# Gate weights and residual rows loaded before the scatter's wait, split before the last silu, and two token tiles transposed from finished rows

## The chip, the cores and the metric

The kernel runs on one core of a Trainium2 chip. The metric is the device time of one execution in microseconds (us). One core has TensorE (PE), VectorE (DVE), ScalarE (ACT), GpSimd (POOL) and SyncE (SP), which here only issues DMA transfers; 16 DMA engines move the data.

## The reference

One hybrid decoder layer on 512 tokens of width 1024, in float32:

```python
h = rms_norm(x, g_mix[i]); proj = h @ w_in[i]
# conv branch and block-sparse attention, normalised, concatenated, projected
x = x + mixed @ w_out[i]                                   # x1
x = x + hier_moe(rms_norm(x, g_ffn[i]), ...)               # x2; top-2 of 8 experts in the top-1 of 4 groups
gate = jax.nn.sigmoid(rms_norm(x, g_ple[i]) @ w_ple_gate[i] + b_ple_gate[i])
x = x + (p[i] @ w_ple_proj[i]) * gate                      # x3
return rms_norm(x, g_final)
# each expert: silu(h @ w_gate[e]) * (h @ w_up[e]) @ w_down[e], with F = 256
```

The change lies where the experts end and the gate product (x2 @ w_ple_gate, 1024 by 1024) begins.

## The kernel before

Every engine has its own program, written out by hand, and semaphores join them; the order of the instructions on an engine is the order in the source.

*Experts.* A tile is 128 rows of gathered tokens, 96 of one expert (a = 0) and 32 of another (a = 1). For tile n TensorE multiplies by the gate and up weights (L1987), ScalarE takes the silu (L1023), VectorE multiplies by the up half (L1567), TensorE turns the result (L2008), ScalarE copies it out (L1028), TensorE multiplies by the down weights (L2017), and ScalarE (L1031) and VectorE (L1573) copy the two halves of the result into yb. GpSimd scatters yb to y_d in memory (L818), by token and by which of its two experts it was. Weights stream into two slots of wring; SP reloads a slot's up weights (L607) when its up product is done, and the down weights (L635) when its down product is done. `before` is the index of the last pair of tiles, so that tile 2 * before + 1 is the last.

*What follows them.* x2 = x1 + gw0 * y0 + gw1 * y1 for four token tiles t. For t = 0 and 1 (BY_PASS) the part of the last expert tile doesn't go through memory: SP loads what y_d holds once the scatter of tile 2 * before is done (`early`, L738), VectorE adds it to x1 to give xp (add_early, L1554), and TensorE adds the last tile's share straight from yb, with a matrix share_of[t] that picks and weighs its rows. turn_and_add gives x2 of such a tile transposed, as 8 pairs of a matmul with the identity (L2077) and one with share_of (L2078); add_in_rows gives the share in rows (L2087), and VectorE adds xp (rows_out, L1604) to give x2 in rows in xs. For t = 2 and 3 (LATE) the last scatter must be done; its issue on POOL waits for the early loads to have landed, since these read what it overwrites. SP then loads yg (L751), VectorE adds twice (add_last, L1554), and TensorE transposes xs (turn_x2, L2064).

*The gate product.* product(q, lo, hi) does passes lo to hi of quantity q (q = half * 4 + t): wpg_hi times x2_hi, wpg_hi times x2_lo, wpg_lo times x2_hi, eight matmuls each (L2052). ScalarE makes wpg_hi (split_gate, L1014) and x2_hi (high_out, L1050), VectorE wpg_lo (L1590) and x2_lo (low_out, L1611). The gate weights of half 0 are loaded in two halves of 1 MB over the up weights of slot 0 (L740), x1 comes back from memory as two pairs of token tiles (L729 and L741), and half 1 of the gate weights follows (L743). Behind the last expert tile 36 turns of the identity keep TensorE occupied (L2090). Behind the product come, for each q, the sigmoid, the multiply with the p projection, the add to xs, and for the later half the final norm and the store.

Of the kernel before, what the change touches and what calls it, by code (L numbers as in the profile page):

```python
# [28 lines left out]
F32 = mybir.dt.float32  # L29
# [7 lines left out]
P = 128  # L37
# [23 lines left out]
BY_PASS = (0, 1)  # L61
LATE = (2, 3)
# [161 lines left out]
def build(nc, x, w_in, w_out, w_r, w_gate, w_up, w_down, w_pg, w_pp, pT, b_pg, g_final, prm, cst, out):  # L224
    ctx = ExitStack()
    with ctx:
# [323 lines left out]
        def _(sp):  # L550
# [179 lines left out]
            sp.wait_ge(down_done, 2 * last_pair + 1)  # L730
            sp.sem_inc(sp_go, 1)
            sp.wait_ge(y_stored[0], 16 * half)
# [6 lines left out]
            for kh, loaded in enumerate((pg_half, pg_loaded[0])):  # L739
                sp.dma_start(wpg[0][:, 4 * kh:4 * kh + 4], pg[:, 4 * kh:4 * kh + 4, 0:512]).then_inc(loaded, 16)  # L740
            sp.dma_start(xs[:, 2:4], x1_rows[:, 2:4]).then_inc(x1_loaded[1], 16)  # L741
# [102 lines left out]
        def _(act):  # L844
# [172 lines left out]
            def one(n, s, h, made, prior=None):  # L1017
                prior = n - 1 if prior is None else prior
                for q in made[:1]:
                    ple_out(q)  # L1020
                act.wait_ge(up_done, n + 1)
# [22 lines left out]
            one(2 * before + 1, 1, before, MADE_LAST[1], 2 * before)  # L1044
# [17 lines left out]
            split_gate(0, 0, 4)  # L1062
            high_out(0)
            split_gate(0, 4, DK)
# [51 lines left out]
        def _(dve):  # L1116
# [440 lines left out]
            def add_early(t):  # L1557

                if t == 0:
                    dve.wait_ge(x1_loaded[0], 16)  # L1560
                for k in range(2):
                    add_rows(xp[:, t, :], xs[:, t, :], early[:, 2 * t + k, :], early_loaded[t], t, k, xp_ready, 2 * t + k)

            def one(n_, s, h, last, prior):
                dve.wait_ge(sil_ready, n_ + 1)
# [3 lines left out]
                if not last:  # L1569
                    x_out(n_ + 1, 1 - s, n_)  # L1570
# [14 lines left out]

            def split_gate(h):

                for k in range(DK):
                    dve.wait_ge(whi_ready, h * DK + k + 1)
                    dve.scalar_tensor_tensor(out=wpg_lo[h][:, k, :], in0=wpg[h][:, k, :], scalar=pr[:, Q_PLE + k:Q_PLE + k + 1],  # L1590
                                             in1=wpg_hi[h][:, k, :].bitcast(F32), op0=ALU.mult,
                                             op1=ALU.subtract).then_inc(wlo_ready, 1)
# [22 lines left out]
            add_early(0)  # L1615
            add_early(1)
            low_out(0)
            rows_out(0)
            split_gate(0)
            low_out(1)  # L1620
            rows_out(1)
# [5 lines left out]
            split_gate(1)  # L1627
# [65 lines left out]
        def _(pe):  # L1693
# [363 lines left out]
            def turn_x2(t):  # L2057
                pe.wait_ge(x2_ready, 2 * LATE.index(t) + 2)
                for kh in range(2):
                    name = ("x2", t, kh)  # L2060
# [6 lines left out]
            def turn_and_add(t):  # L2067

                pe.wait_ge(xp_ready, 2 * t + 2)
                for kh in range(2):  # L2070
                    name = ("x2", t, kh)
                    banks.wait_free(pe, name)
                    if t == 0:
                        pe.wait_ge((ya_ready, yd_ready)[kh], 2 * before + 2)
                    for k in range(4):
                        cols = slice((4 * kh + k) * P, (4 * kh + k + 1) * P)
                        pe.matmul(bk(name)[:, k * P:(k + 1) * P], xp[:, t, cols], ident, start=True, stop=False)  # L2077
                        ins = pe.matmul(bk(name)[:, k * P:(k + 1) * P], yb[:, 1, cols], share_of[t], start=False, stop=True)  # L2078
                    filled(ins, name)

            pe.wait_ge(xgT_ready, 4 * before + 4)
            def add_in_rows(t):

                for kh in range(2):
                    name = ("rows", t, kh)
                    banks.wait_free(pe, name)
                    filled(pe.matmul(bk(name)[:], share_of[t], yb[:, 1, kh * 512:(kh + 1) * 512], start=True, stop=True), name)  # L2087

            for _ in range(36):
                pe.transpose(pb[3][:, 0:P], ident, ident)  # L2090
# [42 lines left out]
```

## Time and profile before

| | us |
|---|---|
| median of 3 runs | 584.43 |
| lowest, highest | 580.81, 585.07 |
| the profiled execution | 582.8 |
| its span | 581.0 |
| TensorE busy in it | 514.4 |
| VectorE busy | 299.1 |
| ScalarE busy | 188.7 |
| DMA, 154.52 MB | mean 266 GB/s |

Times in the rows are counted from the start of the span. A row of the timeline has its start, its length, the engine, the line, the operation and, in brackets, how long the engine had stood idle and what ended that. In the answers on one line of the source the durations are in ns, min/median/max, and behind them stand the first and the last start. A landing is the time from a transfer's issue to its last part's arrival.

### The profile page before, as it was taken

The numbers are of one execution on the slowest core, as the hardware profiler recorded it, in microseconds if no ns is written. First come the engines' busy times: TensorE is split into PE (matmuls) and PEld (weight loads), VectorE is DVE, ScalarE is ACT, GpSimd is POOL, SyncE is SP. The second block draws the span as 40 slices with busy tenths as digits, with TensorE's granted clock in tenths as the row PEclk, the third lists the DMA queues.
The fourth block names the chain that finished last, engine by engine and source line by source line (L and its number), as shares of the span: only waits on it lengthen the run. The fifth ranks groups of instructions, "written<-read, shape, count | busy, mean of one in ns | idle before, by whom it ended". The sixth has DMA issues, their size and how long they took to land.

```text
span 581.0 us, 9043 instructions
## 1 busy us (share of the span) xinstructions
PE 514.4 (89%) x3313; PEld 308.3 (53%) x3313; DVE 299.1 (51%) x577; ACT 188.7 (32%) x361; POOL 78.1 (13%) x90
## 2 busy tenths in 40 slices
PE   4999999997889979988999996969989799899993
PEld 4788888774556658873333332323323223268882
DVE  4339899999996954487232111101111111059866
ACT  6821411337775352331101000101111001146675
POOL 1740000000042040010211221011110200010000
PEclk9999999999889979998999999989989989999998
DMA  9931900445506065498999999999999999596002
GB/s 316 372 130 40 394 21 16 148 158 172 213 2 272 1 260 212 151 392 302 334 395 422 417 421 417 408 386 409 414 418 397 410 397 418 213 396 253 2 36 109
DMA packets 39000, 154.52 MB, mean 266 GB/s; under 512 B 5808, under 2 KB 10416, under 8 KB 27568
## 3 DMA queue, kind: packets, MB, share of 16 engines
q1 hardware_dynamic: 33488, 143.33, 62.8%
q0 software_dynamic: 5184, 10.50, 4.9%
q8 instruction: 26, 0.43, 0.3%
q10 hardware_dynamic: 288, 0.15, 0.1%
q14 instruction: 14, 0.11, 0.1%
HBM read 142.43 MB, written 18.87 MB: 278 GB/s over the span
## 4 chain that ended last, share of the span: by engine, by line
PE 57%; DMA 21%; DVE 9%; ACT 6%; SPq 3%; issue 3%; POOL 1%; DVEq 0%; POOLq 0%; ACTq 0%
DMA wring<-w_up_in 20%; PE bank L1716 15%; PE bank L1987 13%; PE bank L2052 6%; PE bank L1818 5%; PE bank L1742 4%; PE bank L2017 3%; SPq L540 2%; SPq L607 1%; PE bank L1859 1%; PE bank L1786 1%; DVE wring L1239 1%; DVE mix L1176 1%; PE bank L1699 1%; DVE woa_lo L1226 1%
## 5 line engine op out<-in xcount | busy, mean ns | idle before, releaser
L1987 PE MATMUL bank<-wring,arena 128*32 128x512 f32 x848 | 106.7, 633 | 20.7 <-DMA wring<-w_up_in 19.5
L1176 DVE SCALAR_TENSOR_TENSOR mix<-arena,pr,mix 128x512 f32<-128x512 f32 x120 | 86.6, 792 | 0.0
L1987 PEld LDWEIGHTS bank<-wring,arena 128*32 128x32 f32 x848 | 30.9, 116 | 89.6 <-issue 78.9
L1567 DVE TENSOR_TENSOR arena<-arena,bank 128x256 f32<-128x256 f32 x16 | 6.7, 421 | 135.8 <-ACT arena L1023 135.8
L2017 PE MATMUL bank<-wring,arena 128*32 128x512 f32 x448 | 51.0, 595 | 6.8 <-ACT arena L1028 6.8
L1023 ACT ACTIVATE arena<-bank 128x256 f32<-128x256 f32 x16 | 6.1, 384 | 129.7 <-PE bank L1987 129.7
L818 POOL DMA_INDIRECT y_d<-arena,ycur x16 | 16.4, 1026 | 174.4 <-DVE arena L1573 173.4
L1573 DVE COPY arena<-bank 128x512 f32<-128x512 f32 x16 | 11.1, 692 | 54.6 <-PE bank L2017 54.6
L1716 PE MATMUL bank<-hT_hi,win_hi 128*128 128x512 f32 x128 | 33.5, 398 | 1.5 <-DVE hT_lo L1154 0.9
L2017 PEld LDWEIGHTS bank<-wring,arena 128*32 128x32 f32 x448 | 13.2, 109 | 35.2 <-issue 26.6
L1716 PE MATMUL bank<-hT_lo,win_hi 128*128 128x512 f32 x128 | 31.6, 389 | 0.0
L1716 PE MATMUL bank<-hT_hi,win_lo 128*128 128x512 f32 x128 | 31.6, 389 | 0.0
L1031 ACT ACTIVATE arena<-bank 128x512 f32<-128x512 f32 x16 | 9.6, 597 | 60.5 <-PE bank L2017 60.5
L1716 PEld LDWEIGHTS bank<-hT_hi,win_hi 128*128 128x128 f32 x128 | 23.6, 188 | 9.8 <-ACT hT_hi L872 1.9
L1716 PEld LDWEIGHTS bank<-hT_lo,win_hi 128*128 128x128 f32 x128 | 24.0, 188 | 5.0
L1716 PEld LDWEIGHTS bank<-hT_hi,win_lo 128*128 128x128 f32 x128 | 24.0, 188 | 5.0
L775 POOL TENSOR_TENSOR mixa_lo<-mix,mixa_hi 128x512 fp32r<-128x512 f32 x4 | 5.7, 1415 | 134.4 <-ACT mix L933 134.4
L1460 DVE TENSOR_TENSOR arena<-bank,pr 128x512 f32<-128x512 f32 x31 | 20.0, 687 | 5.3 <-PE bank L1950 4.9
L867 ACT ACTIVATE win_hi<-wring 128x1024 fp32r<-128x1024 f32 x20 | 20.0, 1071 | 6.5 <-DMA wring<-w_in_in 6.5
L911 ACT ACTIVATE wring<-wring,nmax 128x128 f32<-128x128 f32 (+3 forms) x32 | 17.8, 560 | 11.0 <-DVE nmax L1239 11.0
L769 POOL TENSOR_TENSOR win_lo<-wring,win_hi 128x1024 fp32r<-128x1024 f32 x8 | 18.9, 2390 | 14.7 <-ACT win_hi L867 14.7
L1950 PEld LDWEIGHTS bank<-c,arena 128*128 128x128 f32 x128 | 13.9, 140 | 12.4 <-issue 11.1
(292 smaller groups left out, 888.8 us busy)
## 6 DMA issues: line engine op xcount, KB each, us to landing
wring<-w_down_in SPq DMA_DIRECT2D x28, 1024.0 KB, 18.5
wring<-w_gate_in SPq DMA_DIRECT2D x24, 1024.0 KB, 12.7
wring<-w_up_in SPq DMA_DIRECT2D x24, 1024.0 KB, 18.3
wring<-w_in_in SPq DMA_DIRECT2D x3, 2048.0 KB, 14.4
wring<-w_in_in SPq DMA_DIRECT2D x4, 1024.0 KB, 11.6
y_d<-rt SPq DMA_DIRECT2D x1, 4096.0 KB, 18.3
wring<-w_out_in SPq DMA_DIRECT2D x2, 2048.0 KB, 9.1
wring<-y_d SPq DMA_DIRECT2D x8, 512.0 KB, 6.3
```

Source lines behind the costliest of these rows:

```text
L769: pool.tensor_tensor(win_lo[j][:, :, cols], win[j][:, :, cols], win_hi[j][:, :, cols].bitcast(F32), ALU.subtract).then_inc(win_lo_ready[j], 1)
L818: pool.indirect_dma_start(y_d, bass.IndirectOffsetOnAxis(ap=ycur[:, s:s + 1], axis=0), yb[:, s, :], None, bounds_check=2 * S - 1, oob_is_e ...
L867: act.activation(win_hi[i][:, :, cols], win[i][:, :, cols], ACT.Copy).then_inc(win_hi_ready[i], 1)
L911: act.activation(prob[:, u_ % 4, hh, 0:n], prob[:, u_ % 4, hh, 0:n], ACT.Exp, scale=-1.0, bias=nmax[:, b, hh:hh + 1], accum_out=psum_p[:, ...
L1176: ins = dve.scalar_tensor_tensor(out=mixc[:, mm, :], in0=u[:, mm, j:j + S], scalar=w, in1=mixc[:, mm, :], op0=ALU.mult, op1=ALU.add)
L1460: dve.tensor_tensor(xgT[:, s, 4 * kh:4 * kh + 4, :], pb[kh][:].rearrange("p (k n) -> p k n", k=4), pr[:, Q_FFN + 4 * kh:Q_FFN + 4 * kh + 4 ...
L1716: ins = pe.matmul(bk(name)[:], w[:, k, m * P:(m + 1) * P], h[:, k, :], start=(j == 0 and k == 0), stop=(j == 2 and k == DK - 1))
L1742: ins = pe.matmul(bk(("v", t))[:], h[:, k, t * P:(t + 1) * P], w[:, k, :], start=(j == 0 and k == 0), stop=(j == 2 and k == DK - 1))
L1818: ins = pe.matmul(bk(name)[:], src[:, m, t * P:(t + 1) * P], weight[:, m, half * 512:(half + 1) * 512], start=(j == 0), stop=(j == 3 * CM ...
L1987: ins = pe.matmul(pb[2 + s][lo:hi, :], xgT[:, s, k, lo:hi], weights[:, :, k, :], start=(k == 0), stop=(k == DK - 1))
L2017: ins = pe.matmul(pb[6 + half][lo:hi, :], hidT[:, s, k, lo:hi], dn_cols(w, a, k, half), start=(k == 0), stop=(k == FK - 1))
L2052: ins = pe.matmul(bk(name)[:], lhs, w[:, k, :], start=(j == 0 and k == 0), stop=(j == 2 and k == DK - 1))
```

## The change

SP's wait for the last but one tile becomes a wait for its up product, and behind it SP issues the two halves of the gate weights and the second pair of x1 at once, ahead of its waits for the scatters and ahead of the early y loads. ScalarE and VectorE split six of the eight slices of the first gate weights (AHEAD = 6) in the last expert tile: ScalarE in front of its wait for the up product and so in front of the silu, VectorE in front of its multiply. VectorE also does the two early adds of tile 0 between its multiply and its copy of the down result. turn_and_add and the 36 idle turns are gone; for t = 0 and 1 TensorE makes the rows first (add_in_rows), VectorE adds xp, and turn_x2 transposes the sum. TensorE's order is rows(0), turn(0), pass 1 of product 0, rows(1), passes 2 and 3, turn(1), product 1 and so on as before.

```diff
--- before.py
+++ after.py
@@ -59,6 +59,7 @@
 MADE = {8: (0,), 9: (1, 2), 10: (3,), 11: (4, 5)}
 MADE_LAST = ((6,), (7,))
 BY_PASS = (0, 1)
+AHEAD = 6
 LATE = (2, 3)
 LAST = 2 * TT - 1
 STRAIGHT = NE // 2 - 4
@@ -727,8 +728,11 @@
             last_pair = pairs_but_last(sp)
             y_rows = y_d.rearrange("(k t p) n -> p t k n", k=2, p=P)
             sp.dma_start(xs[:, 0:2], x1_rows[:, 0:2]).then_inc(x1_loaded[0], 16)
-            sp.wait_ge(down_done, 2 * last_pair + 1)
+            sp.wait_ge(up_done, 2 * last_pair + 1)
             sp.sem_inc(sp_go, 1)
+            for kh, loaded in enumerate((pg_half, pg_loaded[0])):
+                sp.dma_start(wpg[0][:, 4 * kh:4 * kh + 4], pg[:, 4 * kh:4 * kh + 4, 0:512]).then_inc(loaded, 16)
+            sp.dma_start(xs[:, 2:4], x1_rows[:, 2:4]).then_inc(x1_loaded[1], 16)
             sp.wait_ge(y_stored[0], 16 * half)
             sp.sem_inc(sp_go, 1)
             sp.wait_ge(y_stored[1], 16 * last_pair)
@@ -736,9 +740,6 @@
             for t in BY_PASS:
                 for k in range(2):
                     sp.dma_start(early[:, 2 * t + k, :], y_rows[:, t, k]).then_inc(early_loaded[t], 16)
-            for kh, loaded in enumerate((pg_half, pg_loaded[0])):
-                sp.dma_start(wpg[0][:, 4 * kh:4 * kh + 4], pg[:, 4 * kh:4 * kh + 4, 0:512]).then_inc(loaded, 16)
-            sp.dma_start(xs[:, 2:4], x1_rows[:, 2:4]).then_inc(x1_loaded[1], 16)
             banks.wait_full(sp, ("ple", 2 * TT - 1))
             sp.dma_start(wpg[1], pg[:, :, 512:D]).then_inc(pg_loaded[1], 16)
 
@@ -1014,10 +1015,13 @@
                     act.activation(wpg_hi[h][:, k, :], wpg[h][:, k, :], ACT.Copy,
                                    scale=pr[:, Q_PLE + k:Q_PLE + k + 1]).then_inc(whi_ready, 1)
 
-            def one(n, s, h, made, prior=None):
+            def one(n, s, h, made, prior=None, last=False):
                 prior = n - 1 if prior is None else prior
                 for q in made[:1]:
                     ple_out(q)
+                if last:
+                    split_gate(0, 0, 4)
+                    split_gate(0, 4, AHEAD)
                 act.wait_ge(up_done, n + 1)
                 wait(act, hid_ready, prior)
                 act.activation(sil[:, s, :], pb[2 + s][:, 0:F], ACT.Silu).then_inc(sil_ready, 1)
@@ -1041,7 +1045,7 @@
                 for s in range(2):
                     one(2 * i + s, s, i, ())
             one(2 * before, 0, before, MADE_LAST[0], 2 * number(act, halves[0:1, 2:3], PAIRS // 2 - 2, HALVES - 2) + 1)
-            one(2 * before + 1, 1, before, MADE_LAST[1], 2 * before)
+            one(2 * before + 1, 1, before, MADE_LAST[1], 2 * before, True)
 
             def high_out(t):
 
@@ -1059,9 +1063,8 @@
                     act.wait_ge(x2_ready, 2 * LATE.index(t) + 2)
                 mean_root(2, t, junk)
 
-            split_gate(0, 0, 4)
             high_out(0)
-            split_gate(0, 4, DK)
+            split_gate(0, AHEAD, DK)
             high_out(1)
             split_gate(1, 0, 4)
             for kh in range(2):
@@ -1554,19 +1557,31 @@
                 dve.scalar_tensor_tensor(out=to, in0=rows, scalar=gw[:, k, t:t + 1], in1=base if k == 0 else to,
                                          op0=ALU.mult, op1=ALU.add).then_inc(done, 1)
 
-            def add_early(t):
+            def add_early(t, ks):
 
                 if t == 0:
                     dve.wait_ge(x1_loaded[0], 16)
-                for k in range(2):
+                for k in ks:
                     add_rows(xp[:, t, :], xs[:, t, :], early[:, 2 * t + k, :], early_loaded[t], t, k, xp_ready, 2 * t + k)
 
+            def split_gate(h, lo, hi):
+
+                for k in range(lo, hi):
+                    dve.wait_ge(whi_ready, h * DK + k + 1)
+                    dve.scalar_tensor_tensor(out=wpg_lo[h][:, k, :], in0=wpg[h][:, k, :], scalar=pr[:, Q_PLE + k:Q_PLE + k + 1],
+                                             in1=wpg_hi[h][:, k, :].bitcast(F32), op0=ALU.mult,
+                                             op1=ALU.subtract).then_inc(wlo_ready, 1)
+
             def one(n_, s, h, last, prior):
+                if last:
+                    split_gate(0, 0, AHEAD)
                 dve.wait_ge(sil_ready, n_ + 1)
                 wait(dve, hidT_full, prior)
                 dve.tensor_tensor(hid[:, s], sil[:, s, :].rearrange("p (n k) -> p k n", k=FK),
                                   pb[2 + s][:, F:2 * F].rearrange("p (n k) -> p k n", k=FK), ALU.mult).then_inc(hid_ready, 1)
-                if not last:
+                if last:
+                    add_early(0, (0, 1))
+                else:
                     x_out(n_ + 1, 1 - s, n_)
                 dve.wait_ge(down_done, n_ + 1)
                 wait(dve, y_stored[s], 16 * h)
@@ -1583,14 +1598,6 @@
             one(2 * before, 0, before, False, 2 * number(dve, halves[0:1, 2:3], PAIRS // 2 - 2, HALVES - 2) + 1)
             one(2 * before + 1, 1, before, True, 2 * before)
 
-            def split_gate(h):
-
-                for k in range(DK):
-                    dve.wait_ge(whi_ready, h * DK + k + 1)
-                    dve.scalar_tensor_tensor(out=wpg_lo[h][:, k, :], in0=wpg[h][:, k, :], scalar=pr[:, Q_PLE + k:Q_PLE + k + 1],
-                                             in1=wpg_hi[h][:, k, :].bitcast(F32), op0=ALU.mult,
-                                             op1=ALU.subtract).then_inc(wlo_ready, 1)
-
             def add_last(t, k):
 
                 add_rows(xs[:, t, :], xs[:, t, :], yg[:, 2 * t + k, :], yg_loaded[t], t, k, x2_ready, 2 * LATE.index(t) + k)
@@ -1612,19 +1619,19 @@
                         x2_lo[t][:, 4 * kh:4 * kh + 4, :], bk(name)[:].rearrange("p (k n) -> p k n", k=4),
                         x2_hi[:, 4 * kh:4 * kh + 4, t * P:(t + 1) * P].bitcast(F32), ALU.subtract), name)
 
-            add_early(0)
-            add_early(1)
+            rows_out(0)
+            add_early(1, (0,))
             low_out(0)
-            rows_out(0)
-            split_gate(0)
+            add_early(1, (1,))
+            split_gate(0, AHEAD, DK)
+            rows_out(1)
             low_out(1)
-            rows_out(1)
             dve.wait_ge(x1_loaded[1], 16)
             for t in LATE:
                 for k in range(2):
                     add_last(t, k)
             low_out(2)
-            split_gate(1)
+            split_gate(1, 0, DK)
             low_out(3)
             for t in range(TT):
                 inverse(2, t)
@@ -2055,8 +2062,11 @@
                     filled(ins, name)
 
             def turn_x2(t):
-                pe.wait_ge(x2_ready, 2 * LATE.index(t) + 2)
+                if t in LATE:
+                    pe.wait_ge(x2_ready, 2 * LATE.index(t) + 2)
                 for kh in range(2):
+                    if t in BY_PASS:
+                        banks.wait_emptied(pe, ("rows", t, kh))
                     name = ("x2", t, kh)
                     banks.wait_free(pe, name)
                     for k in range(4):
@@ -2064,37 +2074,21 @@
                         ins = pe.transpose(bk(name)[:, k * P:(k + 1) * P], xs[:, t, cols], ident)
                     filled(ins, name)
 
-            def turn_and_add(t):
-
-                pe.wait_ge(xp_ready, 2 * t + 2)
+            def add_in_rows(t):
+
                 for kh in range(2):
-                    name = ("x2", t, kh)
+                    name = ("rows", t, kh)
                     banks.wait_free(pe, name)
                     if t == 0:
                         pe.wait_ge((ya_ready, yd_ready)[kh], 2 * before + 2)
-                    for k in range(4):
-                        cols = slice((4 * kh + k) * P, (4 * kh + k + 1) * P)
-                        pe.matmul(bk(name)[:, k * P:(k + 1) * P], xp[:, t, cols], ident, start=True, stop=False)
-                        ins = pe.matmul(bk(name)[:, k * P:(k + 1) * P], yb[:, 1, cols], share_of[t], start=False, stop=True)
-                    filled(ins, name)
-
-            pe.wait_ge(xgT_ready, 4 * before + 4)
-            def add_in_rows(t):
-
-                for kh in range(2):
-                    name = ("rows", t, kh)
-                    banks.wait_free(pe, name)
                     filled(pe.matmul(bk(name)[:], share_of[t], yb[:, 1, kh * 512:(kh + 1) * 512], start=True, stop=True), name)
 
-            for _ in range(36):
-                pe.transpose(pb[3][:, 0:P], ident, ident)
-            turn_and_add(0)
+            add_in_rows(0)
+            turn_x2(0)
             product(0, 0, 1)
-            add_in_rows(0)
-            product(0, 1, 2)
-            turn_and_add(1)
             add_in_rows(1)
-            product(0, 2, 3)
+            product(0, 1, 3)
+            turn_x2(1)
             for t in range(1, TT):
                 product(t, 0, 2)
                 if t < TT - 1:
```

## Rows read from the trace of the kernel before

**Rows 1.** Chain of waits from 478 us on: start, us, what.

```profile
478.72 18.64 DMA wring<-w_up_in
...
506.35 3.64 PE bank L2017 x32
509.99 4.08 PE bank L2090 x36
514.07 0.22 PE bank L2077 x2
...
521.27 1.72 PE bank L2087 x4
...
530.14 5.48 PE bank L2052 x24
535.62 0.87 PE bank L2064 x8
```

**Rows 2.** Timeline, all engines, 503 to 529 us (parts).

```profile
504.55 0.38 ACT L1023 ACTIVATE arena<-bank 128x256 f32<-128x256 f32 x1 [7.22 <-PE bank L1987]
504.96 0.42 DVE L1567 TENSOR_TENSOR arena<-arena,bank 128x256 f32<-128x256 f32 x1 [9.34 <-ACT arena L1023]
...
510.06 0.60 ACT L1031 ACTIVATE arena<-bank 128x512 f32<-128x512 f32 x1 [3.76 <-PE bank L2017]
510.06 0.69 DVE L1573 COPY arena<-bank 128x512 f32<-128x512 f32 x1 [4.67 <-PE bank L2017]
510.67 1.28 DVE L1554 SCALAR_TENSOR_TENSOR arena<-wring,gw,xs 128x1024 f32<-128x1024 f32 x1
511.50 0.49 POOL L811 COPY ycur<-tlist 128x1 int32 x1 [13.99 <-DMA wring<-y_d]
513.03 1.08 POOL L818 DMA_INDIRECT y_d<-arena,ycur  x1 [1.05 <-issue]
514.01 2.56 ACT L1014 ACTIVATE wpg_hi<-wring,pr 128x512 fp32r<-128x512 f32 x4 [3.36 <-DMA wring<-w_pg_in]
520.25 1.76 SPq L751 DMA_DIRECT2D wring<-y_d  x4
523.64 5.38 DVE L1590 SCALAR_TENSOR_TENSOR wpg_lo<-wring,pr,wpg_hi 128x512 fp32r<-128x512 f32 x8
```

**Rows 3.** Stretches: us, busy by engine, clock, DMA share, GB/s.

```profile
495.00:497.50 2.50, 1.78 (x8) 0.48 (x11) 0.62 (x1) 1.11 (x2) 0.99 (x1) 1.00 0.56 234
497.50:500.00 2.50, 2.50 (x24) 0.71 (x28) 0.00 (x0) 0.00 (x0) 0.01 (x1) 1.00 0.49 192
500.00:505.00 5.00, 4.48 (x44) 1.17 (x36) 0.04 (x1) 0.38 (x1) 0.00 (x0) 1.00 0.24 84
```

**Rows 4.** Landings: L729 (x1), L738 (early y), L740 (gate halves), a down load at 463.

```profile
L729 SPq DMA_DIRECT2D xs<-x_d x1: 388/388/388, 482.7 to 482.7; - x1
...
DMA to landing us min/median/max: 22.8/22.8/22.8
...
L738 SPq DMA_DIRECT2D wring<-y_d x4: 337/424/432, 503.8 to 505.1; - x4
...
DMA to landing us min/median/max: 3.5/4.9/6.2
...
L740 SPq DMA_DIRECT2D wring<-w_pg_in x2: 529/632/736, 505.6 to 506.4; - x2
...
DMA to landing us min/median/max: 8.4/9.5/10.5
...
wring<-w_down_in SPq DMA_DIRECT2D x1, 1024.0 KB, 23.8
```

**Rows 5.** TensorE: two up products, and the clock (0.50) in one of them.

```profile
465.34 8.77 PE L1987 MATMUL bank<-wring,arena 128*32 128x512 f32 x64 [3.92 <-DMA wring<-w_up_in]
...
481.92 7.07 PE L1987 MATMUL bank<-wring,arena 128*32 128x512 f32 x64 [0.39 <-DMA wring<-w_up_in]
...
467.00:469.00 2.00, 2.00 (x12) 0.43 (x8) 0.00 (x0) 0.00 (x0) 0.00 (x0) 0.50 0.96 397
```

More of the change, by code:

```diff
@@ L2065, in turn_x2 @@
                     filled(ins, name)
-            def turn_and_add(t):
-                pe.wait_ge(xp_ready, 2 * t + 2)
-                for kh in range(2):
-                    name = ("x2", t, kh)
-                    banks.wait_free(pe, name)
-                    if t == 0:
-                        pe.wait_ge((ya_ready, yd_ready)[kh], 2 * before + 2)
-                    for k in range(4):
-                        cols = slice((4 * kh + k) * P, (4 * kh + k + 1) * P)
-                        pe.matmul(bk(name)[:, k * P:(k + 1) * P], xp[:, t, cols], ident, start=True, stop=False)
-                        ins = pe.matmul(bk(name)[:, k * P:(k + 1) * P], yb[:, 1, cols], share_of[t], start=False, stop=True)
-                    filled(ins, name)
-            pe.wait_ge(xgT_ready, 4 * before + 4)
             def add_in_rows(t):
@@ L2086, in add_in_rows @@
                     banks.wait_free(pe, name)
+                    if t == 0:
+                        pe.wait_ge((ya_ready, yd_ready)[kh], 2 * before + 2)
                     filled(pe.matmul(bk(name)[:], share_of[t], yb[:, 1, kh * 512:(kh + 1) * 512], start=True, stop=True), name)
-            for _ in range(36):
-                pe.transpose(pb[3][:, 0:P], ident, ident)
-            turn_and_add(0)
+            add_in_rows(0)
+            turn_x2(0)
             product(0, 0, 1)
-            add_in_rows(0)
-            product(0, 1, 2)
-            turn_and_add(1)
             add_in_rows(1)
-            product(0, 2, 3)
+            product(0, 1, 3)
+            turn_x2(1)
             for t in range(1, TT):
```

## Prediction

> **What bounds the kernel now.** I read the chain of waits first, from 478 us to the end [rows 1]. Its first piece is not work of an engine but the transfer of the last expert tile's up weights, which holds everything until 497.36. Then comes the last tile on TensorE: up product, silu, product with the other half, turn, down product, ended at 509.99. From there the chain is TensorE almost without a hole: 36 idle turns (4.08 us), two tiles turned and added from xp and yb, two sets of rows, and 24 passes of the gate product. So an instruction that leaves TensorE between 510 and 572 gives its full time back, if its inputs are there; before 497 only DMA counts.
>
> Second, the timeline around the last tile [rows 2]: its silu runs on ScalarE at 504.55, the multiply on VectorE at 504.96, and neither engine has anything to do for the seven us before. That hole is where the change puts the splits. Third, the DMA share by stretches [rows 3]: full until 495, then 0.56, 0.49 and 0.24, and full again from 505. That looks like room: 2.5 x 0.44 + 2.5 x 0.51 + 5 x 0.76 = 6.2 us of all engines, or 2.5 MB at the 400 GB/s of the full stretches. Fourth, and this decides, the landings [rows 4]. The first x1 transfer (1 MB, L729) is issued at 482.7 and lands after 22.8 us, at 505.4 or 505.5 (I go on with 505.4), though the mean share has been under 0.6 for ten us. A few DMA engines are far behind the rest, and a transfer is complete only when its last part is.
>
> **The change part by part.**
>
> *Removed from TensorE.* The 36 idle turns, 4.08. turn_and_add(0) and (1): each 16 pieces of 0.22, two instructions a piece, like the first of them at 514.07 [rows 1], so 3.6 each. In their place turn_x2(0) and (1), two lots of eight transposes at 0.87 (the row at 535.62 [rows 1]), so 7.2 - 1.7 = 5.5 less. add_in_rows stays at 1.72 each.
>
> *The new head, if down ends when it does now.* Rows of yb need both copies of the down result (ScalarE to 510.66, VectorE to 510.75 [rows 2]). Then rows 1.72; VectorE adds the second half 0.69 (L1604, as the copy of the same shape at 510.06 [rows 2]); the last four transposes 0.5; ScalarE's high part 0.6; what is left of the first pass, with the splits of k 6 and 7 behind that high part (2 x 0.64), some 1.6 with the steps between. That is 5.1 plus 0.7 for the copy, 5.8 to the end of pass 1, at 515.9. Now pass 1 ends at 521.3 (the piece of rows at 521.27 starts there). Behind pass 1 there are now 23 passes x 1.82 (5.48 for three) = 41.9, rows(1) 1.72, and three turns x 0.87 = 2.6: 46.2. The last pass, ended at 571.9 in the profile, would end at 562.1: 9.8 less, before any stall. From the last pass on nothing is touched.
>
> *The moved loads.* SP now waits for the up product of the last tile but one, which ends at 488.99 [rows 5], instead of its down product, some 5.6 us on (in the last tile down ends 5.5 behind up: 509.99 against 504.5). It then issues the two 1 MB halves of the gate weights and the second x1 transfer (1 MB), all three ahead of its waits for the scatters, which end now at 503.8 [rows 4]. Behind them now stand the wait itself (nothing lost, they are issued long before), the four early y loads and the second half of the gate weights. In the queue they stand behind the x1 transfer that lands at 505.4. In the stretch after 503.8 transfers land in the order of issue: early y at 505.1 + 6.2 = 511.3, gate halves at 505.6 + 8.4 = 514.0 and 506.4 + 10.5 = 516.9 [rows 4]. The gate halves cost 2.8 each there. On the parts that are last, the same work comes behind 505.4: first half 508.2, second 511.1. Transfers do not speed up the late parts: the average share is no measure of them.
>
> By the Trainium skill (DMA: Bandwidth & Descriptors, Queues, rings and completion order) each engine consumes its own ring in order, and a DMA's count is full only when each of its engines has posted. The trace agrees: 505.4 at a share of 0.24. By that rule the sum is the one here; by the mean share alone the halves would be there by 503.5.
>
> *The splits in front of the silu.* ScalarE now waits in front of the silu for the first half (508.2; four splits, 2.56, to 510.8) and the second (511.1; two more, 1.28, to 512.4; the four at 514.01 took 2.56 [rows 2]). Queued behind them is the last silu: 512.8 instead of 504.93. VectorE's last low part (5.38 / 8 = 0.67 each, L1590 [rows 2]) ends at 513.1, its multiply at 513.55 instead of 505.38: 8.2 later. Who waits for that: TensorE's turn of hid, the down product, both copies, the scatter and all of the head. TensorE stands still for some 9 us.
>
> *The clock.* After an idle time of 3.92 us at 461.4 the granted clock fell from full (2.4 GHz) to half (1.2) at 467, and the 64 matmuls took 8.77 us instead of 7.07 [rows 5]. A 9 us hole won't cost less than that in kind; the nearest row gives 1.7. The bounds: nothing, if the fall lies wholly in the hole; 4.1, if turn (0.44) and down (3.64) all run at half. I take 1.7. By the Trainium skill (TensorE: Matmul & The Clock Gate, Why this matters for your kernels) waits on DMA between bursts lower the clock, which speaks against this change too; the row has the number.
>
> So down ends at 509.99 + 8.2 + 1.7 = 519.9, pass 1 at 525.8.
>
> *The second scatter and what hangs on it.* The early y loads (2 MB, 5.2 on the late parts) now stand behind the moved x1 transfer (2.6): 511.1 + 2.6 + 5.2 = 518.9 instead of 511.3. The last scatter waits for them (copy and issue 1.5 more [rows 2], 520.4) and for yb (520.6 and 0.9 on POOL as now): issued at 521.5. It needs 7.2 (513.03 to the y loads' issue at 520.25), so 528.7; two y loads 4.9 (median of the early ones), 533.6; VectorE's two adds 2 x 1.28, 536.2. TensorE comes to turn_x2(2) at 525.8 + 1.72 + 2 x 1.82 + 0.87 + 2 x 1.82 = 535.7. A stall of 0.5 us. VectorE's new order (rows_out(0), one add, low_out(0), the other, two splits, rows_out(1)) ends rows_out(1) near 530, before turn_x2(1) at 531.2, so it costs nothing; were it 1 us later, it would cost that. VectorE starts on the gate outputs 1.8 us nearer to the end than now, which I cost at nothing: the outputs come three passes, 5.5 us, apart [rows 1], and it has idle time between the late ones; with that cover gone it costs up to 1.8.
>
> *Sum.* 525.8 + 46.2 + 0.5 = 572.5 against 571.9: the 9.8 saved are given back as 8.2 of late splits, 1.7 of clock and 0.5 of stall, +0.6. The profiled execution has a span of 581.0 and took 582.8; the new one takes 583.4. It stood 1.6 below the median of the runs, 584.4. On that scale I predict 585.
>
> Bounds of this case: with no cost of the clock, down ends at 518.2, but the scatter is then held by the early loads, and the stall grows to 1.1: 572.0 - 0.7 = 571.3, or 583.8 on the median's scale. With 4.1: 587.4. If the late parts are 2 us less late, the whole chain is 2 us earlier: 583. So 582 to 588.
>
> **The rivals.**
>
> *A. The hole in DMA takes the loads in.* If what lags were only the x1 transfer and the moved ones ran in the free share, 2 MB would be in at 503.5, the split of k 5 done at 504.8 and the silu at most 0.4 late. Then early y lands at 511.3 as now, the scatter is done at 520.3, y at 525.2, the adds at 527.8, against TensorE at 515.9 + 0.4 + 9.9 = 526.2: a stall of 1.6. End 515.9 + 0.4 + 46.2 + 1.6 = 564.1, 7.8 less: 576.6 on the median's scale. For it: the share of 0.24. Against it: 22.8 us for x1, and 23.8 for a down load in the loop before [rows 4], which says that the lag is no single event.
>
> *B. The late parts are later still (slower).* Place: the wait for the second half, in front of the silu. If the first half, issued at 489.1, needs what that down load needed, 23.8, it lands at 512.9 and the second at 515.8, 4.7 later than in the sum. With the clock at half through all of the down product (2.4 more) the end is 0.6 + 4.7 + 2.4 = 7.7 over before: 592. It decides (over 590.3) from 5.3 us above my sum on. For it: 2 KB rows in the gate weights against 8 KB in the experts'. Against it: the same halves cost 2.8 each at 511 to 517, beside full traffic.
>
> *C. The lag is partly gone.* The halves land 3 to 5 us earlier than in my sum, and the end with them: 580 to 582, within 1% still.
>
> **How the numbers follow.** The held-back silu as summed 0.5, C 0.12, A 0.25, B 0.13. One per cent of 584.4 (about what a measurement of this kernel can tell from no change) is 5.8: faster is under 578.6, which is A, 0.25; slower is over 590.3, B, 0.13; the rest 0.62. The likeliest case gives 585; its own range is 582 to 588. To leave out no more than 2 in 10 the range reaches to A's number and to the foot of B: 577 to 591.
>
> **What would show it.** Right: a ScalarE idle time before its first split of about 10 us that ends with the gate weights' landing near 508, a second short one; the silu near 512.4; TensorE idle about 9 us before the turn of hid; a granted clock of 0.5 behind it; the span of 36 idle turns gone; turn_x2(2) waiting for less than 2 us. Wrong: the silu within 1 us of 504.6 (then A), a stall of over 3 us at turn_x2(2) (then the scatter was sized wrong), or a full clock through the down product.

## The result, and the profile after

The changed kernel takes 583.8 us in the median (582.35 to 585.93, 20 runs), the kernel before 581.5 (579.93 to 585.07, 20 runs). The ratio is 1.0035, with a 95% interval of 1.0019 to 1.0052: slower by 2.3 us between the medians and 2.0 by the ratio, a small loss that 20 runs can tell, and within 1%. The forecast was 585, range 577 to 591, and "within 1%" as the likeliest.

Chain of waits of the changed kernel from 458 us on (start, us, what):

```profile
458.87 20.38 DMA wring<-w_up_in
...
479.30 7.12 PE bank L1994 x64
...
486.50 19.17 DMA wring<-w_pg_in
...
505.69 0.73 ACT wpg_hi L1015
...
506.45 3.31 DVE wpg_lo L1571 x5
...
512.07 6.33 PE bank L2024 x32
```

Before, the chain stands on the up weights until the last tile and goes straight down the tile [rows 1]. Now it runs through the gate weights, which are no part of that tile: their transfer, ScalarE's split, VectorE's low parts, and only then the multiply and the down product.

Timeline of the changed kernel, the same stretch:

```profile
495.02 7.07 PE L1994 MATMUL bank<-wring,arena 128*32 128x512 f32 x64 [0.95 <-DMA wring<-w_up_in]
...
501.24 1.76 SPq L742 DMA_DIRECT2D wring<-y_d  x4
...
505.69 4.00 ACT L1015 ACTIVATE wpg_hi<-wring,pr 128x512 fp32r<-128x512 f32 x6 [10.99 <-DMA wring<-w_pg_in]
506.45 4.08 DVE L1571 SCALAR_TENSOR_TENSOR wpg_lo<-wring,pr,wpg_hi 128x512 fp32r<-128x512 f32 x6 [13.45 <-ACT wpg_hi L1015]
509.60 0.36 ACT L1027 ACTIVATE arena<-bank 128x256 f32<-128x256 f32 x1
510.44 0.41 DVE L1580 TENSOR_TENSOR arena<-arena,bank 128x256 f32<-128x256 f32 x1
...
510.91 0.69 PE L2015 MATMUL bank<-c,arena 128*128 128x128 f32 x2 [8.82 <-DVE arena L1580]
...
512.07 6.28 PE L2024 MATMUL bank<-wring,arena 128*32 128x512 f32 x32 [0.47 <-ACT arena L1032]
...
513.58 1.28 DVE L1557 SCALAR_TENSOR_TENSOR arena<-wring,gw,xs 128x1024 f32<-128x1024 f32 x1 [2.72 <-DMA wring<-y_d]
...
518.43 0.69 DVE L1588 COPY arena<-bank 128x512 f32<-128x512 f32 x1 [2.25 <-PE bank L2024]
...
519.98 0.98 POOL L819 DMA_INDIRECT y_d<-arena,ycur  x1 [3.56 <-DVE arena L1588]
...
522.73 1.75 SPq L752 DMA_DIRECT2D wring<-y_d  x4
```

The last up product ends at 502.09, and the silu starts at 509.60: 7.5 us later, where [rows 2] has it at once behind. TensorE stands idle for 8.82 us before the turn, and the down product takes 6.28 us instead of 3.64. Four stretches show more (columns as in [rows 3]; the last three numbers are the granted clock, the DMA share and the GB/s):

```profile
498.00:500.00 2.00, 2.00 (x24) 0.65 (x20) 0.00 (x0) 0.00 (x0) 0.00 (x0) 1.00 0.80 299
500.00:502.00 2.00, 2.00 (x20) 0.39 (x12) 0.00 (x0) 0.00 (x0) 0.00 (x0) 1.00 0.75 250
...
508.00:510.00 2.00, 0.00 (x0) 0.00 (x0) 2.00 (x4) 1.85 (x4) 0.00 (x0) 0.50 1.02 412
...
514.00:516.00 2.00, 2.00 (x14) 0.39 (x8) 1.96 (x2) 0.00 (x0) 0.00 (x0) 0.50 0.66 249
```

*The clock.* It falls in TensorE's hole (0.80 from 506 to 508), stands at its half level (1.2 GHz, 0.50) from 508 to 516, and comes back towards the end of the down product (0.64 from 516 to 518).

*The loads.* The executions reach the last up product 2.4 us apart, so the hole of [rows 3] (a share of 0.24 from 500 to 505) has to be looked for some 2.4 us earlier here. There the share is 0.80 and 0.75. The hole was mostly filled, and the weights came late all the same. The landings are:

```profile
L734 SPq DMA_DIRECT2D wring<-w_pg_in x2: 398/2993/5588, 486.5 to 486.9; - x2
...
DMA to landing us min/median/max: 19.2/20.3/21.4
```

The first half, issued at 486.50, was complete at 505.67, the second, issued at 486.94, at 508.33. The trace also has the time at which each of the sixteen parts of a transfer was complete. Of the first half fourteen parts were in by 501.5, before the up product ended, and the last two at 505.5 and 505.7. Of the x1 transfer ahead of it fourteen were in by 498.4 and the last two at 502.8 and 503.0. So it is two parts of sixteen that hold everything. The trace doesn't say which engines carry them; the same lag in each transfer fits the same two engines.

**A measure that leaves the front out.** Up to the last tile the two programs do the same work, but for the loads moved from 486.5 on. Still the executions reach its up product at times some us apart (497.41 and 495.02 here). The effect is therefore also read from that product's start to the end of the span, the tail: 581.0 - 497.41 = 83.6 before, 581.9 - 495.02 = 86.9 after, so +3.3 in these two executions. The moved loads could also delay the last tile's own weights, which the tail would hide. Counted from the up product of the tile before it (481.92 and 479.30), ahead of the moved loads, the effect is +3.5; nearly all of it lies in the tail.

### The profile page after: what moved, and what is told of

Same layout as the page of the kernel before. It is cut to its first block, busy times and chain, and to the rows that moved or that the text cites. A ratio compares the mean times of both kernels' runs of the same rounds, so it can differ in the third digit from the quotient of the medians.

```text
span 581.9 us, 8877 instructions
## 1 busy us (share of the span) xinstructions
PE 507.7 (87%) x3229; PEld 298.9 (51%) x3229; DVE 299.2 (51%) x577; ACT 188.1 (32%) x361; POOL 77.6 (13%) x90
## 4 chain that ended last, share of the span: by engine, by line
PE 57%; DMA 20%; DVE 10%; ACT 7%; issue 3%; SPq 2%; POOL 1%; DVEq 0%; POOLq 0%; ACTq 0%
DMA wring<-w_up_in 15%; PE bank L1723 15%; PE bank L1994 14%; PE bank L2059 5%; PE bank L2024 5%; PE bank L1825 5%; PE bank L1749 4%; DMA wring<-w_pg_in 3%; DMA wring<-w_in_in 2%; SPq L541 1%; PE bank L1866 1%; PE bank L1957 1%; PE bank L1793 1%; DVE wring L1242 1%; DVE mix L1179 1%
## 5 line engine op out<-in xcount | busy, mean ns | idle before, releaser
L1994 PE MATMUL bank<-wring,arena 128*32 128x512 f32 x848 | 106.5, 633 | 20.3 <-DMA wring<-w_up_in 19.1
L1994 PEld LDWEIGHTS bank<-wring,arena 128*32 128x32 f32 x848 | 30.0, 116 | 89.7 <-issue 78.6
L2024 PE MATMUL bank<-wring,arena 128*32 128x512 f32 x448 | 53.6, 621 | 6.8 <-ACT arena L1032 6.8
L2024 PEld LDWEIGHTS bank<-wring,arena 128*32 128x32 f32 x448 | 13.7, 114 | 37.4 <-issue 28.7
L770 POOL TENSOR_TENSOR win_lo<-wring,win_hi 128x1024 fp32r<-128x1024 f32 x8 | 18.9, 2396 | 14.6 <-ACT win_hi L868 14.6
L1793 PE MATMUL bank<-c,wring 128*128 128x128 f32 x80 | 14.1, 311 | 6.6 <-ACT arena L926 6.6
```

Source lines behind the costliest of these rows:

```text
L770: pool.tensor_tensor(win_lo[j][:, :, cols], win[j][:, :, cols], win_hi[j][:, :, cols].bitcast(F32), ALU.subtract).then_inc(win_lo_ready[j], 1)
L1793: ins = pe.transpose(bk(name)[:, j * P:(j + 1) * P], prob[:, b, hh, j * P:(j + 1) * P], ident)
L1994: ins = pe.matmul(pb[2 + s][lo:hi, :], xgT[:, s, k, lo:hi], weights[:, :, k, :], start=(k == 0), stop=(k == DK - 1))
L2024: ins = pe.matmul(pb[6 + half][lo:hi, :], hidT[:, s, k, lo:hi], dn_cols(w, a, k, half), start=(k == 0), stop=(k == FK - 1))
```

## The experiments

All kernels with a ratio, each against runs of the kernel before on the same chip (medians of before: 581.5 beside the changed kernel, 581.39 beside e1 to e4, 581.89 beside the others). The last column compares tails:

| kernel | median us | ratio (95%) | last up product starts | tail us | tail against before |
|---|---|---|---|---|---|
| before | 581.5 | | 497.41 | 83.6 | |
| changed | 583.8 | 1.0035 (1.0019 to 1.0052) | 495.02 | 86.9 | +3.3 |
| e1 splits behind | 589.72 | 1.0142 (1.0106 to 1.0177) | 498.53 | 90.3 | +6.7 |
| e2 gate halves ahead of x1 | 582.27 | 1.0024 (0.9997 to 1.0051) | 494.30 | 83.8 | +0.2 |
| e3 TensorE part alone | 579.74 | 0.9963 (0.9935 to 0.9991) | 495.04 | 82.7 | -0.9 |
| e4 held clock | 581.45 | 1.0015 (0.999 to 1.0039) | 495.89 | 84.0 | +0.4 |
| e5 gate late, splits in front | 591.73 | 1.0169 (1.0126 to 1.0213) | 495.58 | 92.6 | +9.0 |
| e7 splits and adds behind the copy | 582.64 | 1.0007 (0.9984 to 1.003) | 499.88 | 83.9 | +0.3 |
| e9 one half ahead | 575.11 | 0.9878 (0.9845 to 0.991) | 496.93 | 78.6 | -5.0 |
| e10 the same, high part first | 576.15 | 0.99 (0.9867 to 0.9932) | 494.32 | 78.9 | -4.7 |

A median is of 4 to 20 runs, a tail of one execution each. The two give the same order, but for e2, e4 and e7, whose tails lie within 0.2 us of one another; in size they differ by up to 2 us: e9's ratio says 7 us less, its tail 5.0. The intervals of e2, e4 and e7 overlap that of the changed kernel, so what sets these three apart from it rests on their traces.

**The wait made longer (e5).** The loads go back behind the early y, the splits stay in front of the silu:

```diff
             sp.sem_inc(sp_go, 1)
-            for kh, loaded in enumerate((pg_half, pg_loaded[0])):
-                ...
-            sp.dma_start(xs[:, 2:4], x1_rows[:, 2:4]).then_inc(x1_loaded[1], 16)
             sp.wait_ge(y_stored[0], 16 * half)
             ...
                     sp.dma_start(early[:, 2 * t + k, :], y_rows[:, t, k]).then_inc(early_loaded[t], 16)
+            for kh, loaded in enumerate((pg_half, pg_loaded[0])):
                 ...
+            sp.dma_start(xs[:, 2:4], x1_rows[:, 2:4]).then_inc(x1_loaded[1], 16)
```

> The changed kernel with the gate halves and the second x1 issued behind the early y loads, as before the change, but the six splits still in front of the last silu: the suspected wait made longer. Theory (the silu waits for the gate weights): the halves land 9.5 and 12.4 us behind the last up product (514.0 and 516.9 against 504.5 in the trace of before), the silu starts 13.5 us behind it instead of 7.5, and TensorE's idle time is near 15 us; the early adds then no longer hold VectorE's copy, so nearly all of the 6 us shows: 589.5 us, ratio 1.014 (1.009 to 1.018). Rival (the wait is hidden behind something else, such as the y loads): 584, ratio 1.0035.

```profile
512.87 4.02 ACT L1015 ACTIVATE wpg_hi<-wring,pr 128x512 fp32r<-128x512 f32 x6 [17.23 <-DMA wring<-w_pg_in]
...
518.11 0.69 PE L2015 MATMUL bank<-c,arena 128*128 128x128 f32 x2 [15.45 <-DVE arena L1580]
```

The silu came 14.1 us behind the up product (516.79 against 502.65), 6.6 more than in the changed kernel, TensorE idled 15.45 us, and the tail grew by 5.7. The missing 0.9 is the down product, which took 5.36 here instead of 6.28. So the wait in front of the silu is on the path one to one, and the rival is out.

**What stands ahead in the queue (e2).** The first x1 pair is issued behind the gate halves:

```diff
-            sp.dma_start(xs[:, 0:2], x1_rows[:, 0:2]).then_inc(x1_loaded[0], 16)
             sp.wait_ge(up_done, 2 * last_pair + 1)
             sp.sem_inc(sp_go, 1)
             for kh, loaded in enumerate((pg_half, pg_loaded[0])):
                 ...
+            sp.dma_start(xs[:, 0:2], x1_rows[:, 0:2]).then_inc(x1_loaded[0], 16)
```

> The changed kernel with the first x1 transfer (1 MB) issued behind the two gate halves instead of ahead of them; nothing else moved. Theory (late DMA engines work through their queue in order, so what stands ahead decides): both halves land 2.6 us earlier, the silu and the end of the down product come 2.6 us earlier, and 2.2 of it is kept: 581.6 us, ratio 0.9995. Rival (the halves ride in the free share and the x1 transfer beside them doesn't matter): 583.8, ratio 1.0035, landings as before the swap.

Timeline of this kernel:

```profile
494.30 7.07 PE L1994 MATMUL bank<-wring,arena 128*32 128x512 f32 x64 [0.78 <-DMA wring<-w_up_in]
...
502.46 3.98 ACT L1015 ACTIVATE wpg_hi<-wring,pr 128x512 fp32r<-128x512 f32 x6 [8.31 <-DMA wring<-w_pg_in]
...
512.85 1.28 DVE L1557 SCALAR_TENSOR_TENSOR arena<-wring,gw,xs 128x1024 f32<-128x1024 f32 x1 [5.24 <-DMA wring<-y_d]
```

From the last up product's start, the first half was there after 8.2 us instead of 10.7: 2.5 earlier, the price of the 1 MB that no longer stood ahead. All four 1 MB transfers tell the same. Counted from that start they are complete, in the changed kernel, as first x1 pair 8.0, first half 10.7, second half 13.3, second x1 pair 15.9; and here as first half 8.1, second half 10.8, first x1 pair 13.3, second x1 pair 15.9. The place in the queue sets the landing in these two kernels, whichever transfer stands in it. e4, with the loads of the changed kernel, repeats its numbers (8.1, 10.7, 13.4, 15.9).

The tail is 3.1 shorter, of which 0.6 is a down product that took 5.72 instead of 6.28. In the medians the gain on the changed kernel is 1.5 us, but in the ratios only 0.1% (1.0024, where 0.9995 was expected), and the intervals overlap. The landings are shown; how much of them reaches the time is not.

**The clock (e4).** TensorE turns the identity during its wait:

```diff
+                if last:
+                    for _ in range(72):
+                        pe.transpose(pb[2][:, 0:P], ident, ident)
                 pe.wait_ge(hid_ready, n + 1)
```

> The changed kernel with 72 turns of the identity (8.1 us) on TensorE between the last up product and its wait for the multiply. Theory (the idle time lowers the clock, which costs 2.9 us in turn and down product): the down product takes 3.64 us instead of 6.28, the turn 0.44 instead of 0.69; 2.2 us are kept, because VectorE's early adds then stand in front of its copy: 581.6 us, ratio 0.9995. Rival (the long down product has another cause, such as contention with the loads): down stays at 6.3 us, 583.8, ratio 1.0035.

```profile
502.89 8.08 PE L2010 MATMUL bank<-c 128*128 128x128 f32 x72
...
512.75 3.64 PE L2027 MATMUL bank<-wring,arena 128*32 128x512 f32 x32 [0.47 <-ACT arena L1032]
```

The silu still came 7.6 us late (510.52 against 502.96), but the down product was back at 3.64. The loads beside it are the same. So 2.9 us of the changed kernel (2.64 in down, 0.25 in the turn) is the half clock, and not contention with the loads. The tail is 2.9 shorter, the median 2.3.

**The splits behind (e1), which failed.** Loads as in the changed kernel, all eight splits behind the first high part on ScalarE, and VectorE's low parts behind its adds (only ScalarE's lines are shown):

```diff
-                if last:
-                    split_gate(0, 0, 4)
-                    split_gate(0, 4, AHEAD)
 ...
             high_out(0)
-            split_gate(0, AHEAD, DK)
+            split_gate(0, 0, 4)
+            split_gate(0, 4, DK)
```

> The changed kernel with its loads where they are, but all splits of the first gate weights behind the last tile (behind the first high part on ScalarE, behind the early adds on VectorE). Theory (the last silu waits for the gate weights): the silu follows the up product within 0.1 us again, TensorE's idle time of 8.8 us and the half clock behind it are gone, and the down product ends some 11 us earlier. Most of that isn't gained, since VectorE's copy of the down result stands behind the two early adds of tile 0, whose data land where they did (513.6 in the changed kernel's trace): the copy at 516.9 instead of 519.1. 581 us, ratio to before 0.999 (0.995 to 1.001). Rival (the TensorE part itself loses, the wait is hidden): as the changed kernel, 583.8, ratio 1.0035.

I expected 581, and it took 589.7. The silu came at once behind the up product again, and down ended at 511.1, but:

```profile
517.15 1.28 DVE L1555 SCALAR_TENSOR_TENSOR arena<-wring,gw,xs 128x1024 f32<-128x1024 f32 x1 [10.65 <-DMA wring<-y_d]
...
519.68 0.68 DVE L1584 COPY arena<-bank 128x512 f32<-128x512 f32 x1
...
520.51 2.05 PE L2080 MATMUL bank<-arena,rt 128*128 128x512 f32 x2 [7.49 <-DVE arena L1584]
...
525.79 5.04 PE L2055 MATMUL bank<-wpg_hi,x_hi 128*128 128x512 f32 x8 [1.34 <-ACT wpg_hi L1015]
```

VectorE waits for early y in front of its copy of the down result; the early y stands behind 3 MB of moved loads and comes 11.5 us behind the end of the up product. So TensorE idles 7.49 us in the new place. On top of that, eight splits in a row (5.00 us) pace the first pass, which takes 5.04 us. The granted clock reads 0.50 from 516 to 532. My expectation had the first of these three; it had left out the splits in front of the pass and the half clock after the new hole. In the changed kernel the silu's wait had covered the wait for early y and six of the eight splits.

**The same with that taken away (e7).** The six splits of both engines and VectorE's early adds stand behind the copies:

```diff
-                if last:
-                    add_early(0, (0, 1))
-                else:
+                if not last:
                     x_out(n_ + 1, 1 - s, n_)
 ...
+            split_gate(0, 0, AHEAD)
+            add_early(0, (0, 1))
             rows_out(0)
```

> The changed kernel, loads where they are, with the six splits of both engines and VectorE's two early adds all behind the copies of the last down result, ahead of the first rows' addition. Theory (in the run with the splits behind, the early adds stood in front of VectorE's copy and the eight splits in front of the first pass; both are taken away here): counted from the end of the last up product, the copy is done at 6.2 us, the early y is in at 11.5, rows are finished at 15, pass 1 ends at 18.5, against 22.9 in the changed kernel and 16.8 before: 4.4 us under the changed kernel, 579.5 us, ratio 0.9965 (0.993 to 1.000). Rival (something else in the changed loads costs, a slower end of the last tile or of the scatter): 584 or more, ratio 1.0035.

```profile
518.46 1.28 DVE L1556 SCALAR_TENSOR_TENSOR arena<-wring,gw,xs 128x1024 f32<-128x1024 f32 x1 [0.61 <-DMA wring<-y_d]
...
521.84 1.97 PE L2071 MATMUL bank<-c,xs 128*128 128x128 f32 x8 [6.61 <-DVE xs L1606]
```

The tail is 83.9, 3.0 under the changed kernel, where 4.4 were expected; in the medians it is 1.2 under. The half clock (0.50 from 520 to 526; 1.97 for eight turns, against 1.03 where they run at full clock) took a part again. TensorE waits 6.61 us for finished rows, these wait for the early adds, and these for early y. That comes 0.61 us behind the end of VectorE's six low parts, which are close to being the next limit. With the changed loads the TensorE part gains nothing over the kernel before (1.0007); with the loads of before it gains a little (e3, next).

**The TensorE part alone (e3).** Splits as in e1, loads as before:

> The TensorE part of the change alone: rows first, turned from the finished rows, no idle turns; the gate weights and the second x1 are loaded behind the early y loads and split behind the last tile, as before the change. Theory (the TensorE part is sound and the front is what gives it back): the silu stands behind the up product, pass 1 of the first product waits for the splits (halves landing at 514.0 and 516.9) and ends near 519.5, 1.5 to 2 us of wait at the third turn for y; 4.4 us less than before: 577, ratio 0.992 (0.989 to 0.996). Rival (turning from finished rows costs as much as it saves): 581.5, ratio 1.000 or more.

```profile
512.51 0.60 ACT L1051 ACTIVATE x_hi<-bank 128x512 fp32r<-128x512 f32 x1 [0.41 <-PE bank L2070]
...
513.00 5.00 ACT L1015 ACTIVATE wpg_hi<-wring,pr 128x512 fp32r<-128x512 f32 x8
...
513.81 5.04 PE L2055 MATMUL bank<-wpg_hi,x_hi 128*128 128x512 f32 x8 [1.34 <-issue]
```

It gains, but 1.7 us in the medians and not the expected 4.4. Rows are finished early, yet pass 1 takes 5.04 us behind the eight splits instead of 1.98, and the rows and the pass behind it ran at half clock or partly so (3.62 and 3.07 us; 0.50 from 516 to 522, 0.84 to 524). The direction was right, the size was not.

**A version that beats both (e9).** One gate half ahead, then the first x1 pair; early y; the second gate half and x1 pair behind it. The four splits of the first half fill the time of the down product:

```diff
             sp.sem_inc(sp_go, 1)
-            for kh, loaded in enumerate((pg_half, pg_loaded[0])):
-                ...
-            sp.dma_start(xs[:, 2:4], x1_rows[:, 2:4]).then_inc(x1_loaded[1], 16)
+            sp.dma_start(wpg[0][:, 0:4], pg[:, 0:4, 0:512]).then_inc(pg_half, 16)
+            sp.dma_start(xs[:, 0:2], x1_rows[:, 0:2]).then_inc(x1_loaded[0], 16)
 ...
+                if last:
+                    split_gate(0, 0, 4)
                 act.wait_ge(down_done, n + 1)
```

> Loads: only the first gate half ahead of the scatters' wait, the first x1 pair behind it, then early y, the second gate half, the second x1 pair. Four splits behind the silu and the turn's copy (ScalarE) and behind the multiply (VectorE), the early adds behind VectorE's copy, splits 4 to 7 behind the first high part. Theory: from the last up product's end, first half in at 0.2, early y of tile 0 at 5.4 and of tile 1 at 8.0, second half at 10.8; pass 1 ends at 14 (before: 16.8, changed kernel: 22.9); with 46 us of TensorE behind it and 1 to 2 of stall the kernel ends 5 us under before: 576.5 us, ratio 0.9915 (0.987 to 0.996). Rival (what TensorE gave up in idle turns and additions is bounded by transfers in any order): ratio 0.996 as the TensorE part alone.

```profile
505.72 2.55 ACT L1015 ACTIVATE wpg_hi<-wring,pr 128x512 fp32r<-128x512 f32 x4
...
505.87 3.64 PE L2022 MATMUL bank<-wring,arena 128*32 128x512 f32 x32 [0.47 <-ACT arena L1029]
...
513.58 1.26 PE L2072 MATMUL bank<-c,xs 128*128 128x128 f32 x8 [1.30 <-DVE xs L1608]
...
515.01 3.52 PE L2057 MATMUL bank<-wpg_hi,x_hi 128*128 128x512 f32 x8 [0.18 <-ACT x_hi L1053]
...
515.42 2.57 ACT L1015 ACTIVATE wpg_hi<-wring,pr 128x512 fp32r<-128x512 f32 x4
```

575.1 us, 1.2% under the kernel before (0.9845 to 0.991). The first half is complete 8.1 us from the up product's start, as in e2, so the first four splits run beside the down product and nothing waits for them. TensorE's longest wait in these rows is 1.30 us, and the granted clock stays at 1.00. The other four splits (515.42) still pace the first pass, which takes 3.52 us where the later ones take 1.98. Loads, splits and adds differ from the changed kernel together here; what each gives by itself is not shown.

**The high part first (e10).** e9 with high_out(2) ahead of the two roots on ScalarE:

> The kernel with one half ahead, and besides ScalarE makes the high part of tile 2 ahead of the two roots of tiles 0 and 1 (with their table load) instead of behind them. Theory (in the changed kernel the first pass of tile 2 waits 0.74 us for that high part, which ScalarE starts 1.9 us after it could): 0.7 to 1 us less than the kernel with one half ahead alone, 575.7 us, ratio 0.990. Rival (tile 2 waits for y in that kernel, or the roots are then late for VectorE): no difference.

```profile
535.87 1.07 ACT L1053 ACTIVATE x_hi<-bank 128x512 fp32r<-128x512 f32 x2
...
536.59 2.08 PE L2057 MATMUL bank<-wpg_hi,x_hi 128*128 128x512 f32 x8 [0.96 <-ACT x_hi L1053]
```

No gain: the tail is 78.9 against 78.6. In e9 tile 2's pass waited only 0.26 us for its high part, not 0.74, so there was less to win than expected. It no longer waits, but tile 3's does, 0.96 us, because the roots and splits, pushed back, now stand in front of its high part. The wait was moved, not removed. The ratio came out as expected (0.990) by luck: it was built on an e9 of 0.9915, and e9 was 0.9878 already.

## Why the prediction was right, step by step

Times here are counted from the start of the last up product (497.41 before, 495.02 after), so that the earlier front of the execution after is left out.

**The reading that decided.** "In the queue they stand behind the x1 transfer that lands at 505.4": the first half was predicted at 508.2, 10.8 on, and the second at 511.1, 13.7 on; they were complete 10.7 and 13.3 on, behind an x1 transfer complete 8.0 on in both kernels. The free share (case A) would have had both halves in 6.1 on. By 6.5 on fourteen of the sixteen parts of the first half were in; the other two needed 4 us more. e2 (2.5 us earlier for 1 MB less ahead) shows that the queue sets the landing, e5 that the landing sets the silu.

**The splits in front of the silu.** The silu was predicted at 15.0 and measured at 14.6, the end of the multiply at 16.1 and 15.8. The second half was complete at 508.33, just as the first four splits ended, so the predicted second short wait did not show.

**The clock.** Predicted 1.7, with 4.1 as the bound; measured 2.9, and e4 gives this part back (2.9 in the tail). This is the term of the sum that was too small: the nearest row was a hole of 3.92 us, the new one is 8.82.

**The head.** From the down product's end to the end of pass 1 I had 5.9; it took 6.6 (518.35 to 524.97). TensorE's new order did what was said: no idle turns, no turn_and_add.

**The third turn.** I predicted 0.5 us of waiting for y. There was none: the last scatter was done 2.75 us behind its issue (519.98 to 522.73), not 7.2, at a DMA share of 0.17 from 520 to 523. The stall was elsewhere and 1.1 long (0.74 in the row below and 0.34 at tile 1):

```profile
538.29 1.06 ACT L1054 ACTIVATE x_hi<-bank 128x512 fp32r<-128x512 f32 x2
...
539.01 2.09 PE L2059 MATMUL bank<-wpg_hi,x_hi 128*128 128x512 f32 x8 [0.74 <-ACT x_hi L1054]
```

ScalarE makes the roots of tiles 0 and 1 first, with a table load, and so is late for tile 2 (0.74). At tile 1 the turn now stands directly in front of the pass that needs its high part, so TensorE waits for ScalarE there (0.34). The sum had no term for either.

**The sum.** Predicted +0.6, measured +3.3 in the two traces and +2.3 in the medians: 1.2 too little for the clock, 0.7 for the head, 0.6 net at the turns, the rest small gaps, against 0.3 too much for the splits. 9.8 us of work was taken from TensorE and more than that given back in front of it (7.9 by the late silu and 2.9 by the clock). One bound has a slip: by its own terms the end without a cost of the clock is 518.2 + 5.9 + 46.2 + 1.1 = 571.4, not 571.3; nothing hangs on it.

**The scale.** The number 585 was made by putting the profiled execution 1.6 under the median of 3 runs. Over 20 runs the median is 581.5, and the profiled 582.8 stands 1.3 over it. Two misses of opposite sign, the effect too small and the base too high, make the printed number look better than its parts.

## What to carry to other kernels

Before you move a load up in a full queue, read the landing of what stands ahead of it, not the mean share. Here the first gate half was issued 16.7 us earlier, counted from the last up product's start, and was complete only 5.9 us earlier.

Work that fills an idle engine belongs behind the instruction that others wait for, and only as much of it as its data allow. Six splits in front of the silu held it 7.5 us; four behind it, with their loads ordered to suit, held neither the silu nor the down product.

When a wait is removed, the next one may have been covered by it: e1 took the silu's away and was slower for what stood behind.

## What the hardware showed that I had not expected

*SP can be held in the issue itself.* Three 1 MB transfers issued at once behind the first x1 transfer, in the changed kernel:

```profile
486.50 6.03 SPq L734 DMA_DIRECT2D wring<-w_pg_in  x2
...
492.57 7.33 SPq L735 DMA_DIRECT2D xs<-x_d  x1
```

The same kind of transfer takes 0.5 to 0.7 us to issue before [rows 4]. In the first row one of the two issues took 0.40 us and the other 5.59. In both orders the hold began with the third of the four 1 MB transfers: the second gate half here (5.59 us), the first x1 pair in e2 (9.72 us). In e9, where two stand there instead of four, the issues took 0.40 and 0.53. Here SP was free again at 499.9, 1.3 us before the early y's turn, so it cost nothing; one more transfer could have. No run isolates what SP waits for.

*The scatter's time goes with the traffic beside it*: 7.0 to 7.6 us from its issue to the y loads at a share near 1 (before, e3, e9, e10), 4.2 to 4.4 us at a low share but with 3.4 to 3.7 us still to go until the last gate weights landed (e1, e2, e4, e7), and 2.75 us where these had 1.1 us to go or had landed (the changed kernel and e5).

*The clock can fall without a long hole.* In e3 TensorE was busy for 3.5 of the 6 us from 508 to 514, was never idle there for more than 1.34 us, and the granted clock was 0.50 from 516 on. In e9 it was busy for 3.9 of the same 6 us, and the clock stayed at 1.00. No run shows what decides between the two.
